# Moving four of twelve adaLN modulation jobs to later steps of a hybrid attention / MoE kernel

## The reference, cut to what matters

```python
def ada_modulation(cvec, w, b):
    m = jax.nn.silu(cvec) @ w + b
    return jnp.split(m, 6, axis=-1)
...
        sh1, sc1, g1, sh2, sc2, g2 = [m[:, None, :] for m in ada_modulation(c, ada_w[l], ada_b[l])]
        csh1, csc1, cg1, csh2, csc2, cg2 = ada_modulation(c_ctx, ada_w[l], ada_b[l])
...
        x = layer_norm(DN_ALPHA * x + g1 * (ox @ w_out[l]), ln1_g[l], ln1_b[l])
```

## Time and the profile before

| | |
|---|---|
| median of 3 runs | 1444.9 us (1443.07 to 1446.66) |
| profiled execution, its own time | 1440.97 us |
| its span, first to last instruction | 1439.0 us |
| PE busy | 1288.8 us, 90% |
| DVE / ACT / POOL busy | 543.9 / 292.8 / 301.8 us |
| mean granted TensorE clock | 0.949 |
| layer 0's attention steps | about 209 to 379 us |

### The profile page before, as it was taken

The page is one execution under the profiler, slowest core; times in us unless marked ns, Lnnn a source line. Parts: engine busy times, 40 slices in busy tenths (PEclk is TensorE's granted clock), DMA queues, the critical chain, the costliest instruction groups (busy, mean ns, idle before and its releaser), DMA issues.

```text
span 1439.0 us, 19064 instructions
## 1 busy us (share of the span) xinstructions
PE 1288.8 (90%) x6356; PEld 704.4 (49%) x6357; DVE 543.9 (38%) x1327; ACT 292.8 (20%) x715; POOL 301.8 (21%) x394
## 2 busy tenths in 40 slices
PE   5999995999978999989989969899987699999994
PEld 1443452444444666655656724466544354545451
DVE  5303532446575322222323216546446521211124
ACT  0100112323211222222222221212511111111110
POOL 1001002244204233323323300101710411111110
PEclk9999997989988999999999989999988799999997
DMA  9875308535326899999999569340422999999960
GB/s 335 320 277 192 146 0 265 207 144 204 123 100 233 327 374 379 359 369 378 368 383 389 203 260 397 98 166 26 108 103 73 381 401 397 402 408 396 406 250 30
DMA packets 113084, 373.30 MB, mean 259 GB/s; under 512 B 17979, under 2 KB 24381, under 8 KB 104793
## 3 DMA queue, kind: packets, MB, share of 16 engines
q1 hardware_dynamic: 89112, 313.50, 58.1%
q0 software_dynamic: 23008, 55.40, 10.5%
q10 hardware_dynamic: 864, 3.15, 0.5%
HBM read 368.77 MB, written 30.47 MB: 277 GB/s over the span
## 4 chain that ended last, share of the span: by engine, by line
PE 41%; DMA 11%; SPq 9%; DVE 3%; issue 3%; ACT 1%; POOL 0%; POOLq 0%; DVEq 0%; ACTq 0%
PE bank L1335 11%; SPq L647 7%; PE bank L1357 6%; PE bank L1367 5%; DMA weights<-in_exp_w 3%; DMA probs_T<-in_exp_w 3%; PE bank L1323 3%; PE bank L943 3%; DMA qkv<-in_exp_w 2%; PE bank L1145 2%; PE bank L951 2%; PE bank L1036 1%; PE bank L1026 1%; PE bank L1188 1%; DMA a_q<-scratch_y 1%
## 5 line engine op out<-in xcount | busy, mean ns | idle before, releaser
L1335 PE MATMUL bank<-weights,b_qk 128*64 128x256 f32 (+2 forms) x1040 | 160.7, 385 | 1.8 <-DVE b_qk L2295 1.5
L1335 PEld LDWEIGHTS bank<-weights,b_qk 128*64 128x64 f32 (+2 forms) x1040 | 110.7, 147 | 62.3 <-issue 34.5
L2301 DVE TENSOR_TENSOR expert_act<-silu_a,bank 128x128 f32<-128x128 f32 x76 | 21.9, 288 | 309.1 <-ACT silu_a L1658 309.1
L1367 PE MATMUL bank<-tokens_h,a_k 128*128 128x512 f32 x208 | 103.2, 620 | 0.0
L1357 PE MATMUL bank<-weights,expert_act_T 128*64 128x512 f32 (+2 forms) x260 | 92.2, 622 | 10.0 <-DMA weights<-in_exp_w 5.4
L2532 POOL DMA_INDIRECT shift_scale_gate_norm<-scratch_h,gather_index x82 | 85.0, 1037 | 70.6 <-POOL gather_index L2529 43.7
L1335 PE MATMUL bank<-features_h,b_qk 128*32 128x256 f32 (+2 forms) x512 | 95.2, 381 | 0.4
L1323 PE MATMUL bank<-tab,shift_scale_gate_norm 128*128 128x128 f32 x624 | 82.9, 276 | 8.2 <-DMA shift_scale_gate_norm<-scratch_h,gather_index 8.2
L1145 PE MATMUL bank<-weights,features_h 128*128 128x512 f32 x192 | 86.4, 606 | 0.8 <-ACT features_h L1445 0.8
L2485 POOL TENSOR_SCALAR probs<-probs,prob_recip 128x512 f32<-128x512 f32 (+1 forms) x36 | 48.5, 1356 | 176.9 <-DVE prob_recip L2026 176.8
L1658 ACT ACTIVATE silu_a<-bank 128x128 f32<-128x128 f32 x76 | 21.1, 278 | 313.4 <-PE bank L1335 310.3
(11 more groups left out here) (360 smaller groups left out, 1963.2 us busy)
## 6 DMA issues: line engine op xcount, KB each, us to landing
weights<-in_exp_w SPq DMA_DIRECT2D x195, 512.0 KB, 11.7
features_h<-in_exp_w SPq DMA_DIRECT2D x64, 512.0 KB
qkv<-in_exp_w SPq DMA_DIRECT2D x64, 512.0 KB
shift_scale_gate_norm<-in_ada_w SPq DMA_DIRECT2D x24, 1024.0 KB, 8.1
a_q<-in_exp_w SPq DMA_DIRECT2D x32, 512.0 KB
weights<-in_w_in SPq DMA_DIRECT2D x6, 2048.0 KB
shift_scale_gate_norm<-scratch_mod POOLq DMA_DIRECT2D x16, 512.0 KB, 8.8
c_padded<-in_ada_w SPq DMA_DIRECT2D x8, 1024.0 KB, 6.0
```

The source lines that it names most:

```text
L1335: mm = pe.matmul(ab[r, 0:2 * HIDDEN].rearrange("p (m h) -> p m h", m=2), XGT[:, u.slot() % 2, k, r], expert_w13(slot)[:, :, k, :], start=k ...
L1367: mm = pe.matmul(ACC[g][h][:, :], GROW[:, u.slot() % 2, g * P:(g + 1) * P], YSB[:, u.slot() % 2, h * HALF:(h + 1) * HALF], start=False, st ...
```

## The change

Jobs 1, 2, 3 and 4 move from steps 6, 8, 10 and 12 to steps 9, 10, 12 and 13. Jobs 0 and 5 to 11 stay. PE, DVE, and the order in which banks are handed out all follow this list; SP's list of DMAs stays in its order, but the waits in it are on the jobs.

```diff
-ADA_JOBS = (4, 6, 8, 10, 12, 14, 15, 17, 18, 20, 21, 23)
+ADA_JOBS = (4, 9, 10, 12, 13, 14, 15, 17, 18, 20, 21, 23)
```

## The result

The changed kernel takes 1430.21 us (median of 4 runs, 1428.58 to 1431.20) against 1443.99 for the kernel before on the same chip (4 runs, 1441.48 to 1446.66): ratio 0.9902, 95% interval 0.9878 to 0.9925, so 14.1 us (10.8 to 17.6) faster. The forecast was 1432.4 us, a gain of 12.5 us. The profiled execution took 1431.2 us with a span of 1429.1.

What follows compares the result with a forecast made beforehand. PE, busy 90%, was taken as the bound, with its 14.2 us wait on a full DMA queue; second product 11.7 us earlier plus 0.8 makes 12.5, so 1444.9 - 12.5 = 1432.4 us, range 1428 to 1440.

Steps and rivals of the forecast that it cites:

- The wait and its filler: Job 1: PE's 14.23 us wait for block 3 is filled by steps 6 to 8 and the 7.0 us first product.
- The start of the first product: Tile 0, after steps 6 to 8: 4.9 us of work and 2.4 us idle put it at 240.2 us.
- the idle time of the bare steps: Steps 6 to 8 without a job: PE idles 0.8 us in each of three, 2.4 us in all.
- The landing of `w_out`: DMA queue: first half lands at 237 us, second at 245, both before their products need them.
- The rival of the late `w_out`: First product waits for its half landing at L; gain 250.3 - L, 7.3 us at L 243: 1437.6 us; chance 0.12.
- Job 2's wait and the clock: Step 10: PE idles about 2.4 us for block 5, then half-rate clock costs 1.6 us.
- The second product's end: Tile 0, behind job 2: ends at 265.9 us, 11.7 us earlier than before.
- Steps 11 to 13: Behind the second product: job 3 mostly fills PE's idle time; the 11.7 us carry on, plus 0.8 us.
- a longer chain: Steps 11 to 13: DVE's chain exceeding 17.2 us was named as a sign the prediction was wrong.
- The sum: Whole kernel: 11.7 + 0.8 = 12.5 us gained, giving 1432.4 us; chance 0.70.
- the larger gain: Rival: no clock loss behind job 2, less idle in bare steps; 16.5 us gained, 1428.4 us; chance 0.10.
- the wait that only moves: Rival: job 1 still waits and steps 11 to 13 give the gain back, 1444.9 us; no-change cases together 0.05.

Runs made afterwards that it cites:

- e1: Changed kernel with job 1 in step 8, ahead of the first output product, not step 9; ratio 0.9936 to the kernel before, median 1434.0 us.
- e4: Kernel before with its own job list; SP issues the second half of `w_out` ahead of its wait for the convolution; ratio 0.9949 to the kernel before.
- e2: Changed kernel with jobs 3 and 4 in steps 11 and 12, not 12 and 13; ratio 0.9903 to the kernel before, 1430.4 us.
- e6: Changed kernel with job 2 in step 11, jobs 3 to 6 in steps 13 to 16, columns in step 14; ratio 0.9920 to the kernel before.
- e8: The job list and columns of e6, plus the second half of `w_out` issued ahead of the wait for the convolution; ratio 0.9904 to the kernel before.
- e10: Changed kernel plus the second half of `w_out` issued ahead of the wait for the convolution; ratio 0.9874 to the kernel before, median 1424.9 us.
- e9: Changed kernel with only job 2 moved, to step 11 behind the second product; ratio 0.9892 to the kernel before, 1428.2 us.
- e7: Changed kernel with SP issuing the second half of `w_out` ahead of the first; ratio 0.9954 to the kernel before.
- e5: Changed kernel run once more, nothing altered; ratio 0.9905 to the kernel before, median 1428.3 us.
- e11: Changed kernel with jobs 1 to 4 in steps 8, 9, 11 and 13, and the second half of `w_out` issued early; ratio 0.9899 to the kernel before.

## Why the prediction held

*The wait and its filler.* Right. Block 3's wait went from 14.23 to 0.50 us; e1 shows that the product is about half of the gain. e4 shows that the transfers of `w_out` ahead of the block are what it waits for: with one of the two halves out of its way it came 7.3 us earlier.

*The start of the first product.* Forecast for 240.2 on the clock of before; it started 13.6 us behind job 0, at 239.9. That this fits so well is luck in part, for three terms inside it were off and made up for each other: the idle time of the bare steps was 0.72 and 0.43 us, 1.15 in all, in place of 2.4; their work was 5.4 us in place of 4.9; and 0.53 us of wait stands before the product itself.

*The landing of `w_out`.* The weakest step. 237 us was estimated for the first half from the bytes moved. In e2 the product waited for it until 14.1 us behind job 0, which is 240.4; in e6, e8 and e10 it started without any wait at 12.9, 239.2. So it lands within about a microsecond of when it is needed, where the prediction had counted on 3 us to spare; that it came in time was luck. The 0.53 us in the change is put down to an ACT copy into `c_padded`, which the product doesn't read. In e6 the product starts at 238.51, before the same copy begins (238.61), so the copy can't be what holds it. In e6 and e9, whose kernels are the same up to there, block 3 was in use 21.6 and 22.2 us behind job 0 without a wait, where the change waited for it until 22.8 and e2 until 23.4. So the queue as a whole was later, by 0.6 us and more, in the executions in which the product waited. It is then probably `w_out` that the product waited for, but that is argued and not shown. The second half was right: 245 estimated, 245.6 for that place in e7. The rival of the late `w_out`, with its loss of 1 us for each us, began right where the change stands, and e7 bears its formula out within about 1 us (4.7 against 5.8).

*Job 2's wait and the clock.* 2.4 us forecast, 2.34 measured, with block 5 landing 5 us after its issue as in the earlier trace rows. The half clock behind it was charged with 1.6 us, and the rows show that: 0.50 at 255 to 257 us, 1.54, 1.12 and 1.12 us in place of 1.04, 0.66 and 0.66, and 0.2 in the product. The price came back in nearly every kernel with such a wait. Here are the four groups of matmuls behind the wait (the last is the product, in e9 scores):

| kernel | wait | matmuls behind it, us | at full rate | lost |
|---|---|---|---|---|
| the change | 2.34 | 1.54, 1.12, 1.12, 7.25 | 1.06, 0.66, 0.66, 7.03 | 1.6 |
| e5 | 2.54 | 1.06, 1.12, 1.12, 7.76 | the same | 1.7 |
| e2 | 2.43 | 1.39, 1.12, 1.12, 7.41 | the same | 1.6 |
| e7 | 2.24 | 1.36, 1.12, 1.12, 7.43 | the same | 1.6 |
| e11 | 2.59 | 1.06, 0.78, 1.12, 8.13 | the same | 1.7 |
| e9 | 2.44 | 1.07, 1.03, 1.11, 1.88 | 1.06, 0.66, 0.66, 1.13 | 1.6 |
| e10 | 2.32 | 1.06, 0.66, 0.66, 7.03 | the first row's | 0.0 |

The Trainium skill (TensorE: Matmul & The Clock Gate, section HAM oscillation) puts the fall down to waits between bursts; six of these seven traces agree, e10 doesn't.

*The second product's end.* 11.7 us earlier forecast, 11.63 measured (51.29 to 39.66).

*Steps 11 to 13.* 0.8 us more forecast, 0.75 measured (12.38 at T1). The size was right, but not the way. Job 3 was to fill PE's idle time; it added 1.9 us of work to the stretch from the second product to T1, and PE's idle time in it fell only from 1.8 to 1.1 us. The larger part came from the clock: its mean in this stretch is 0.92 where it was 0.77 (the rows below), and the scores and both blocks of job 5 ahead of T1 take 1.40, 1.06 and 1.04 us in place of 2.08, 1.94 and 1.69. The prediction named less half-rate clock as a possible small extra. The stretch in the kernel before and then in the changed one, with the columns of the earlier trace rows:

```profile
277.59:300.04 22.45, 20.64 (x153) 10.49 (x153) 17.92 (x44) 8.17 (x27) 10.60 (x7) 0.77 0.30 103
264.42:286.12 21.70, 20.58 (x170) 10.85 (x170) 18.50 (x45) 8.52 (x27) 9.87 (x7) 0.92 0.56 203
```

Timeline of DVE in the changed kernel, against the earlier trace rows:

```profile
264.60 0.69 DVE L1876 TENSOR_TENSOR filters<-bank,shift_scale_gate_norm 128x512 f32<-128x512 f32 x1 [6.64 <-PE bank L1145]
...
280.52 0.73 DVE L2036 TENSOR_SCALAR mod_rows<-bank,tab 128x512 f32<-128x512 f32 x1
...
282.50 1.28 DVE L2018 TENSOR_REDUCE neg_max<-bank 128x1 f32<-128x512 f32 x2
```

DVE's chain is 17.9 us long (264.60 to 282.50) where it was 17.2, by the 0.73 us read of job 4 (L2036). The prediction had that read in its working and yet called a longer chain a sign of being wrong; the sign came, and it cost less than the clock gave back. Of the waits inside, the 0.9 us forecast for block 9 did not come: it was issued at 269.27 and needed at 274.37, 5.1 us later and not 4.3, because the scores between took 1.77 us and PE waited 0.39 for POOL. `columns` waited 0.73 for DVE, 0.5 forecast. That this stretch follows DVE is borne out by e6 from the other side. That jobs 3 and 4 could stand anywhere in it is not: e2 lost 1.4 us there by moving them one step forward.

*The sum.* 12.5 us forecast; 12.2 and 12.5 at T3 in two profiles, 14.1 and 13.7 by the timed ratios with intervals that hold 12.5. The rivals: the larger gain didn't come; the wait that only moves was there in small (2.3 us), with its price already in the sum; nothing was slower.

## What to carry to other kernels

When an engine waits for a transfer that a full queue holds back, look in the program order behind the wait for work that doesn't need it, and move the waiting job behind the longest piece of it; then count what the jobs behind it, now closer together, wait for. Do this with the landing of every transfer that the moved-up work needs, since it may be in the same queue. A start brought forward is worth something only if the engine that takes over next has been waiting for it: e6 brought a product 7 us further forward than the change and had nothing left of it in the end.

## What had not been expected

Layer 0's expert stage, which no experiment touches, has two lengths. From the first gathered rows (L1323) to the first routed sums (L943), in the changed kernel and then in its repetition e5 (minimum, median and longest duration, first and last start):

```profile
L1323 PE MATMUL bank<-tab,shift_scale_gate_norm x624: 272/274/452, 460.2 to 1398.7; 128*128 128x128 f32 x156
L943 PE MATMUL bank<-a_q,probs_T x32: 592/592/1192, 833.9 to 882.3; 128*128 128x512 f32 x32
```

```profile
L1323 PE MATMUL bank<-tab,shift_scale_gate_norm x624: 272/274/449, 460.9 to 1394.6; 128*128 128x128 f32 x156
L943 PE MATMUL bank<-a_q,probs_T x32: 592/592/1190, 831.6 to 880.3; 128*128 128x512 f32 x32
```

That is 373.7 and 370.7 us for the same kernel. The kernel before, e1 and e11 took 369.8 to 370.1, and e2, e4 and e6 to e10 373.3 to 373.7. From 460 to 760 us of the changed kernel DMA's share is 0.93 to 1.00. The 3.6 us by which this stage is longer there than in the kernel before, less the 1.5 us by which job 0 lay earlier, account for the profiled spans differing by only 9.9 us (1439.0 to 1429.1) where T3 shows 12.2. It is also why differences of 2 to 3 us between the experiments are read from their traces. What decides between the two lengths stays open; no experiment was made on it.

Waits of 2.2 to 2.6 us brought the granted clock down in six kernels, and one of 2.32 us in e10 did not. The waits of 0.5 us that PE had shortly before, ahead of the first product and of block 3 in the change, don't tell them apart: e9 and e11 have neither, and their clock fell as well. What was different in e10 stays open.
